# A transformer block's first attention: who inverts the sums of the exponentials

## The chip, the core and the metric

The kernel runs on one core of a Trainium2 chip. A core has five engines with instruction streams of their own: TensorE (PE, matmuls and transposes into PSUM), VectorE (DVE), ScalarE (ACT), GpSimd (POOL) and SyncE (SP, which issues the transfers). They meet only in semaphores: an instruction raises one when it is done, another waits for a value of it. The metric is the time of the whole program on the device in microseconds.

## The reference

Two transformer blocks follow one another on a sequence of 1024 tokens, 1024 wide. Only the attention of the first one bears on the change. It has 8 query heads of 64, and 2 heads of keys and values. Each query block of 128 tokens sees all 1024 keys:

```python
def blocked_gqa(q, k, v):
    q = q * jnp.asarray(1.0 / math.sqrt(HEAD_DIM), q.dtype)
    qb = q.reshape(B, nb, Q_BLOCK, N_KV_HEADS, Q_PER_KV, HEAD_DIM).transpose(1, 0, 2, 3, 4, 5)

    def one_block(qblk):
        s = jnp.einsum('bqkgd,bskd->bkgqs', qblk, k).astype(jnp.float32)
        p = jax.nn.softmax(s, axis=-1).astype(v.dtype)
        return jnp.einsum('bkgqs,bskd->bqkgd', p, v)
...
```

All of it is float32. Before it stand a norm, the input projections and a rotary embedding; behind it the output projection, a gated feed-forward network with a short convolution, and the second block, whose own attention has another shape.

## The kernel before

Almost everything outside the attentions is a large matmul in three products of high and low halves (L746), for which GpSimd splits the weights (L537 to L540).

In the first attention the work is a row of 64 units. A unit is one head of one query block: 128 queries against 1024 keys. Sixteen units (two query blocks) are a pass; three passes run in a hardware loop and the fourth is written out. A unit u goes through these steps:

- TensorE, `scores` (L833): four matmuls of 128x512 into half u%2 of `acc`. They wait until the exponentials of unit u-2 have read that half.
- VectorE, `largest` (L1812): scales the scores in place and finds the bias of the softmax, NBI.
- ScalarE, `exponents` (L1258): the exponentials EX, with their sum in SUM[u%2]. In the trace that is an ACTIVATE and behind it the reading of the accumulator (ACTIVATION_READ_ACCUMULATOR).
- VectorE, `invert_sums` (L1818): RC = 1 / SUM, one element a partition.
- GpSimd, `normalise` (L569, L570): multiplies EX by RC, 16 columns by one form of instruction and 1008 by another.
- TensorE (L863): eight transposes of EX into PSUM, four to a half, in three banks that take turns (`turn`, `bank`). A half needs the bank to be free, that is, the low part PTL of the third half before it.
- ScalarE (L1270) copies a half out rounded, PTH; VectorE (L1842) subtracts to get the low half PTL.
- TensorE, `values` (L848): every second unit sixteen matmuls of PTH and PTL with the values.

Every engine's order is written out by hand, in a loop over u. VectorE at step u: `invert_sums(u+1)`, `largest(u+2)`, at u = 5, 9, 13 the gathering of the output (L1828, L1829), the two halves of PTL of unit u, and at u = 5 and 13 a step of other work (a row of modulations, L1655, here "ADA step"). The fourth gathering stands at the end of the pass. GpSimd at step u: `normalise(u+1)`, then at u = 1 to 3 and 9 to 11 one of three steps in which the queries of the next block are stacked (`stack_queries`: QL at L552, two halves of QST at L560), and at u = 12 and at the end of the pass the low part ML of the output (L587), which waits for the gathered output and ScalarE's rounded copy of it. TensorE takes the units in pairs: for odd u scores(u+2), transposes(u), scores(u+3), transposes(u+1), values(u).

Of the kernel before, what the change touches and what calls it, by code (L numbers as in the profile page):

```python
# [11 lines left out]
ALU = mybir.AluOpType  # L12
# [88 lines left out]
for _name, _w in _VECS:  # L101
    VCOL[_name] = NVEC
    NVEC += _w
_CONSTS = [("ident", 128), ("headmean", 128), ("rot", 128), ("headsel", 2), ("one", 1), ("eps", 1), ("zero", 1), ("edge", 64)]
CCOL, NCONST = {}, 0
for _name, _w in _CONSTS:
    CCOL[_name] = NCONST
# [27 lines left out]
def build(nc, A, out):  # L135
    ctx = ExitStack()
    with ctx:
        BASE = 16512

        def at(name, kb, shape, dt=F32):  # L140
            return nc.alloc_sbuf_tensor_at(name, shape, dt, offset=BASE + int(kb * 1024))

        def sem(name):
            return ctx.enter_context(nc.semaphore(name))
# [16 lines left out]
        EX = [at(f"EX{s}", kb, [P, T]) for s, kb in enumerate((64, 68, 16, 20))]  # L161
# [91 lines left out]
        SUM = at("SUM", small + 1.46875, [P, 8])  # L253
        RC = at("RC", small + 1.5, [P, 8])
# [7 lines left out]
        def con(name, w, j=0):  # L262
            return CON[:, CCOL[name] + j:CCOL[name] + j + w]

        ident, one, eps, zero = con("ident", P), con("one", 1), con("eps", 1), con("zero", 1)
# [33 lines left out]
        scores_done, nb_ready, exp_done, rc_ready, exn_ready = (  # L299
            sem("scores_done"), sem("nb_ready"), sem("exp_done"), sem("rc_ready"), sem("exn_ready"))  # L300
# [27 lines left out]
        def block_of(k):  # L328
            return slice(k, k + 1) if isinstance(k, int) else bass.ds(k, 1)
# [197 lines left out]
        def _(pool):  # L527
# [36 lines left out]

            def normalise(it, u):

                pool.wait_ge(rc_ready, it * 16 + (u + 1))
                x, r = EX[u % 4], RC[:, u % 2:u % 2 + 1]
                pool.tensor_tensor(x[:, 0:FEW], x[:, 0:FEW], r.to_broadcast([P, FEW]), ALU.mult).then_inc(exn_ready, 1)  # L569
                pool.tensor_scalar(x[:, FEW:], x[:, FEW:], r, 1.0, ALU.mult, ALU.mult).then_inc(exn_ready, 1)  # L570

            def attend(it, last):
                for u in range(16):
                    if u < 15 or not last:
                        normalise(it, u + 1)
                    if 1 <= u <= 3:
                        stack_queries(it, 1, u - 1, it * 32 + (2 * u + 4))
                    if 9 <= u <= 11 and not last:
                        stack_queries(it, 2, u - 9, it * 32 + (2 * u + 4))
                    if u == 12:  # L580
                        branch_second(it, 0)
                branch_second(it, 1)
# [8 lines left out]
            for step in range(3):  # L591
                stack_queries(0, 0, step)
            normalise(0, 0)
            with steps.loop(3, 2) as it:
                attend(it, False)
# [987 lines left out]
        def _(dve):  # L1583
# [69 lines left out]
            def modulation(w, cond, out):  # L1653

                ins = dve.scalar_tensor_tensor(out=w, in0=w, scalar=1.0, in1=cond[:, :], op0=ALU.mult, op1=ALU.mult, accum_out=out)  # L1655
                ins.then_inc(ada_used, 1)
# [152 lines left out]
            def largest(it, u):  # L1809
                j = u % 2  # L1810
                dve.wait_ge(scores_done, it * 16 + (u + 1))
                dve.tensor_scalar(acc[:, j, :], acc[:, j, :], column(RSN, it * 16 + u), None, ALU.mult, ALU.min,  # L1812
                                  accum_out=NBI[:, j:j + 1]).then_inc(nb_ready, 1)

            def invert_sums(it, u):
                j = u % 2
                dve.wait_ge(exp_done, it * 16 + (u + 1))
                dve.reciprocal(RC[:, j:j + 1], SUM[:, j:j + 1]).then_inc(rc_ready, 1)  # L1818

            def gather_o(it, b):  # L1820

                dve.wait_ge(otmp_ready, it * 4 + (b + 1))
                g = b % 2
                if g == 0:
                    dve.wait_ge(ml_ready, it * 2 + (b // 2 + 1))
                o = bank6[0:64, :].rearrange("p (i j q) -> p i j q", j=2, q=P)
                m = OTMP[0:64, :].rearrange("p (i j q) -> p i j q", j=2, q=P)
                link(dve.tensor_tensor(OT[0:64, 2 * g:2 * g + 2, :], o[:, :, 0, :], m[:, :, 0, :], ALU.add))  # L1828
                dve.tensor_tensor(OT[64:128, 2 * g:2 * g + 2, :], o[:, :, 1, :], m[:, :, 1, :], ALU.add).then_inc(o_ready, 1)  # L1829

            def attend(it, last):
                for u in range(16):
                    if u < 15 or not last:
                        invert_sums(it, u + 1)
                    if u < 14 or not last:
                        largest(it, u + 2)
                    if u % 4 == 1 and u > 1:
                        gather_o(it, u // 4 - 1)

                    for h in range(2):  # L1840
                        dve.wait_ge(pth_ready, it * 32 + (2 * u + h + 1))
                        dve.tensor_tensor(PTL[:, 4 * h:4 * h + 4, u % 4, :],  # L1842
                                          turns[(2 * u + h) % 3].rearrange("p (k q) -> p k q", q=P),
                                          PTH[:, 4 * h:4 * h + 4, u % 4, :].bitcast(F32), ALU.subtract).then_inc(ptl_ready, 1)
                    if u % 8 == 5:
                        j = u // 8
                        dve.wait_ge(ada3_in[j], it * 16 + 16)
                        modulation(ADA3[j][:, :], C1B, MOD1[:, block_of(it * 2 + (16 + j))])
                gather_o(it, 3)

            dve.wait_ge(cond_ready, 4)
            largest(0, 0)
            largest(0, 1)
            invert_sums(0, 0)
            with steps.loop(3, 4) as it:
                attend(it, False)
            attend(3, True)
            link(dve.tensor_copy(MX[:, 6:7], eps))
            link(dve.tensor_tensor(MOD1[:, 16:24], MOD1[:, 16:24], vec("b_ada", 16, 8), ALU.add))
# [336 lines left out]
def layout(x):  # L2196
# [39 lines left out]
    con = np.zeros((P, NCONST), np.float32)  # L2236
    con[:, CCOL["ident"]:CCOL["ident"] + P] = np.eye(P)
    r = np.arange(P)
    con[:, CCOL["headmean"]:CCOL["headmean"] + P] = (r[:, None] // HD == r[None, :] // HD) / HD
    rot = np.zeros((P, P))  # L2240
# [5 lines left out]
    con[:, CCOL["rot"]:CCOL["rot"] + P] = rot  # L2246
    con[:, CCOL["headsel"]:CCOL["headsel"] + 2] = r[:, None] // HD == np.arange(2)[None, :]
    con[:, CCOL["one"]] = 1.0
    con[:, CCOL["eps"]] = EPS
    for g, w in enumerate(POOL_W):  # L2250
        t = np.r_[0:8, T - 8:T]
# [51 lines left out]
```

## Time and profile before

| | |
|---|---|
| median of 3 runs | 2469.54 us (2466.7 to 2470.85) |
| the profiled execution | 2466.74 us |
| its span | 2465.0 us |
| TensorE busy | 2343.0 us (95%) |
| VectorE busy | 1113.7 us (45%) |
| ScalarE busy | 775.2 us (31%) |
| GpSimd busy | 863.9 us (35%) |
| first attention, from 206 to 418 us: TensorE, VectorE, ScalarE, GpSimd busy | 183.1, 185.8, 163.4, 113.8 us of 212 |

The profile is one execution with the start and length of each instruction. A time in brackets behind an instruction is how long its engine stood idle before it, and what ended that. A row with xN holds several instructions of one form. Busy time of TensorE is that of its matmuls, whose ends are modelled. The span is the time from the first instruction to the last; the execution's own time is a little longer.

### The profile page before, as it was taken

To read this page: it belongs to the slowest core of one execution; us is meant where nothing else is said; L and a number is where in the kernel's file an instruction comes from. 1 tells how busy PE (TensorE), PEld (TensorE's weight loads), DVE (VectorE), ACT (ScalarE), POOL (GpSimd) and SP (SyncE) were. 2 spreads that over 40 slices of the span, in tenths; PEclk is the share of its full clock that TensorE was granted. 3 is DMA by queue.
4 is the path that set the end of the run, shared out by engine and by line. 5 is a ranking of instruction groups with operands and counts; after the bars stand their busy time and mean duration, and the time that the engine had idled before them with its cause. 6 is when DMAs were issued, how large, how long until landed. Compare 5 with 4: busy or idle time off the path is not lost.

```text
span 2465.0 us, 30785 instructions
## 1 busy us (share of the span) xinstructions
PE 2343.0 (95%) x11310; PEld 1924.1 (78%) x11310; DVE 1113.7 (45%) x1381; ACT 775.2 (31%) x1095; POOL 863.9 (35%) x851
## 2 busy tenths in 40 slices
PE   4997888999999999999999999999999999999997
PEld 3776777777888888888778888887778888888886
DVE  7978887479631344124463343352211122222324
ACT  3237776032310222024424454452112111212210
POOL 1445554334433333223223323332223334333331
PEclk9998999999999999999999999999999999999999
DMA  7310001524111111111131111112011111111132
GB/s 305 116 50 28 17 26 49 217 94 179 51 51 43 51 51 43 51 60 49 39 111 61 55 36 54 36 30 91 22 40 44 49 51 52 51 47 41 49 128 77
DMA packets 48318, 166.02 MB, mean 67 GB/s; under 512 B 4480, under 2 KB 6272, under 8 KB 48128
## 3 DMA queue, kind: packets, MB, share of 16 engines
q1 hardware_dynamic: 48256, 165.19, 19.3%
q8 instruction: 39, 0.64, 0.1%
q14 instruction: 23, 0.19, 0.0%
HBM read 156.79 MB, written 8.39 MB: 67 GB/s over the span
## 4 chain that ended last, share of the span: by engine, by line
PE 80%; DVE 9%; issue 4%; ACT 3%; POOL 2%; DMA 1%; SPq 0%; DVEq 0%; ACTq 0%; POOLq 0%
PE acc L746 62%; PE turn L971 6%; PE bank L1035 3%; DVE ADA L1655 1%; DMA WF<-in_w 1%; PE bank L1013 1%; PE acc L959 1%; PE bank L848 1%; DVE HL L1635 1%; DVE acc L1812 1%; PE turn L640 1%; ACT EX L1258 1%; PE acc L724 1%; PE bank L1110 1%; PE bank L1107 1%
## 5 line engine op out<-in xcount | busy, mean ns | idle before, releaser
L746 PE MATMUL acc<-HH,WH 128*128 128x512 f32 x1600 | 497.4, 392 | 7.3 <-POOL WL L540 6.3
L746 PE MATMUL acc<-HL,WH 128*128 128x512 f32 x1600 | 493.9, 390 | 0.0
L746 PE MATMUL acc<-HH,WL 128*128 128x512 f32 x1600 | 493.8, 390 | 0.0
L537 POOL TENSOR_TENSOR WH<-WF,CON 128x16 fp32r<-128x16 f32 x186 | 52.7, 284 | 1206.1 <-PE acc L746 1024.5
L540 POOL TENSOR_TENSOR WL<-WF,WH 128x1024 fp32r<-128x1024 f32 (+2 forms) x186 | 439.5, 2363 | 15.5
L746 PEld LDWEIGHTS acc<-HH,WH 128*128 128x128 f32 x1600 | 300.5, 188 | 74.0 <-issue 6.9
L746 PEld LDWEIGHTS acc<-HL,WH 128*128 128x128 f32 x1600 | 301.3, 188 | 62.8
L746 PEld LDWEIGHTS acc<-HH,WL 128*128 128x128 f32 x1600 | 301.1, 188 | 62.8
L538 POOL TENSOR_SCALAR WH<-WF 128x1008 fp32r<-128x1008 f32 (+2 forms) x186 | 195.4, 1050 | 0.0
L1942 DVE SCALAR_TENSOR_TENSOR CV<-EV,VEC,CV 128x1023 f32<-128x1023 f32 x44 | 99.1, 2253 | 203.9 <-ACT CV L1334 203.1
L1870 DVE SCALAR_TENSOR_TENSOR XT<-acc,MOD,XT 128x1024 f32 (+1 forms) x34 | 43.6, 1284 | 233.1 <-PE acc L746 233.1
L1332 ACT ACTIVATE EV<-acc 128x1024 f32<-128x1024 f32 x44 | 45.2, 1027 | 282.6 <-PE acc L746 276.7
L2127 DVE TENSOR_TENSOR CV<-EV,EV 128x1024 f32<-128x1024 f32 x16 | 33.5, 2096 | 185.5 <-ACT EV L1559 185.5
L746 PE MATMUL acc<-GH,WH 128*128 128x512 f32 x340 | 106.0, 393 | 4.3 <-DVE GL L1958 3.7
L746 PE MATMUL acc<-GL,WH 128*128 128x512 f32 x340 | 105.2, 391 | 0.0
L746 PE MATMUL acc<-GH,WL 128*128 128x512 f32 x340 | 105.2, 390 | 0.0
L2015 DVE TENSOR_TENSOR acc<-acc,BIAS 128x384 f32<-128x384 f32 x64 | 36.1, 564 | 143.0 <-PE acc L962 142.8
L611 POOL TENSOR_TENSOR EX<-EX,RC 128x16 f32<-128x16 f32 x64 | 13.9, 217 | 231.7 <-DVE RC L2021 231.6
L1035 PE MATMUL bank<-PT,VTOK 128*64 128x128 f32 x640 | 84.6, 280 | 0.4 <-DVE CBF L2031 0.4
L1812 DVE TENSOR_SCALAR_CACHE_REDUCE acc<-acc,RSN 128x1024 f32<-128x1024 f32 x64 | 82.3, 1287 | 3.0 <-PE acc L833 0.5
L1258 ACT ACTIVATE EX<-acc,NBI 128x1024 f32<-128x1024 f32 x64 | 71.5, 1117 | 30.6 <-DVE acc L1812 30.0
L746 PEld LDWEIGHTS acc<-GH,WH 128*128 128x128 f32 x340 | 63.9, 189 | 19.0 <-DVE GL L1958 4.9
(373 smaller groups left out, 4100.2 us busy)
## 6 DMA issues: line engine op xcount, KB each, us to landing
WF<-in_w SPq DMA_DIRECT2D x150, 512.0 KB, 3.4
ADA<-in_ada SPq DMA_DIRECT2D x15, 1024.0 KB, 13.1
BIAS<-in_bias SPq DMA_DIRECT2D x16, 576.0 KB, 3.8
XT<-in_xT SPq DMA_DIRECT2D x16, 512.0 KB, 10.2
ADA<-in_ada SPq DMA_DIRECT2D x4, 2048.0 KB, 11.6
ADA<-in_ada SPq DMA_DIRECT2D x3, 2560.0 KB, 9.3
WF<-in_w SPq DMA_DIRECT2D x24, 256.0 KB, 2.6
ADA<-in_ada SPq DMA_DIRECT2D x8, 512.0 KB, 3.4
```

Source lines behind the costliest of these rows:

```text
L537: pool.tensor_tensor(h[:, 0:FEW], f[:, 0:FEW], zero.to_broadcast([P, FEW]), ALU.add).then_inc(w_hi, 1)
L538: pool.tensor_scalar(h[:, FEW:k * P], f[:, FEW:k * P], 1.0, 1.0, ALU.mult, ALU.mult).then_inc(w_hi, 1)
L540: pool.tensor_tensor(WL[slot][:, 0:k, :], WF[slot][:, 0:k, :], WH[slot][:, 0:k, :].bitcast(F32), ALU.subtract).then_inc(w_split, 1)
L746: last = pe.matmul(acc[:, slot, HALF * c:HALF * c + HALF], w[slot][:, k, :], x[:, k, HALF * c:HALF * c + HALF], start=(k == 0 and w is WH ...
L971: mm = pe.matmul(turn[:, HALF * c:HALF * c + HALF], w[slot][:, k, :], x[:, k, HALF * c:HALF * c + HALF], start=(k == 0 and w is WH and x i ...
L1035: mm = pe.matmul(bank7[0:HD, P:2 * P], VTOK2[:, j, kc, :], PT2[u % 2][:, P * k:P * k + P], start=(k == 0), stop=(k == NKEY // P - 1))
L1258: act.activation(EX[u % 4][:, :], acc[:, u % 2, :], ACT.Exp, bias=NBI[:, u % 2:u % 2 + 1], scale=-1.0, accum_out=SUM[:, u % 2:u % 2 + 1]). ...
L1332: act.activation(EV[s][:, :], acc[:, s, :], ACT.Copy).then_inc(act_step, 1)
L1812: dve.tensor_scalar(acc[:, j, :], acc[:, j, :], column(RSN, it * 16 + u), None, ALU.mult, ALU.min, accum_out=NBI[:, j:j + 1]).then_inc(nb_ ...
L1870: dve.scalar_tensor_tensor(out=x, in0=acc[:, s, :], scalar=gate(it * 2 + s), in1=x, op0=ALU.mult, op1=ALU.add).then_inc(acc_read, 1)
L1942: link(dve.scalar_tensor_tensor(out=CV[s][:, 1:T], in0=EV[s][:, 0:T - 1], scalar=vec("conv_w", f), in1=CV[s][:, 1:T], op0=ALU.mult, op1=AL ...
L2015: link(dve.tensor_tensor(a[:, P:P + NLOC], a[:, P:P + NLOC], BIAS[g % 2][:, KIND[c], :], ALU.subtract))
```

## The change

GpSimd computes the inverse itself: `normalise` now waits for the exponentials (`exp_done`), raises SUM to the power of -1 (a new constant, one column `minus` of the table of constants), waits for its own result through the same semaphore `rc_ready`, and multiplies as before. `invert_sums` and its calls are gone from VectorE's stream. The second attention keeps its reciprocals on VectorE.

```diff
-_CONSTS = [("ident", 128), ("headmean", 128), ("rot", 128), ("headsel", 2), ("one", 1), ("eps", 1), ("zero", 1), ("edge", 64)]
+_CONSTS = [("ident", 128), ("headmean", 128), ("rot", 128), ("headsel", 2), ("one", 1), ("eps", 1), ("zero", 1), ("edge", 64), ("minus", 1)]
...
             def normalise(it, u):
 
+                x, r = EX[u % 4], RC[:, u % 2:u % 2 + 1]
+                pool.wait_ge(exp_done, it * 16 + (u + 1))
+                pool.tensor_tensor(r, SUM[:, u % 2:u % 2 + 1], con("minus", 1), ALU.pow).then_inc(rc_ready, 1)
                 pool.wait_ge(rc_ready, it * 16 + (u + 1))
-                x, r = EX[u % 4], RC[:, u % 2:u % 2 + 1]
...
-            def invert_sums(it, u):
-                j = u % 2
-                dve.wait_ge(exp_done, it * 16 + (u + 1))
-                dve.reciprocal(RC[:, j:j + 1], SUM[:, j:j + 1]).then_inc(rc_ready, 1)
-
...
                 for u in range(16):
-                    if u < 15 or not last:
-                        invert_sums(it, u + 1)
                     if u < 14 or not last:
                         largest(it, u + 2)
...
             largest(0, 1)
-            invert_sums(0, 0)
```

GpSimd's stream in a pass, from the normalising of unit 2 to that of unit 4, with the stacking between (EX_63 to EX_66 are the four tiles of exponentials, QST_56 the stacked queries). Before:

```order
L569 TENSOR_TENSOR EX_65<-EX_65,RC 128x16 [waits rc_ready]
L570 TENSOR_SCALAR EX_65<-EX_65,RC 128x1008
L551 ISA
L552 ISA [waits qh_ready]
L552 TENSOR_TENSOR QL<-QN,QH 128x512
L567 REGISTER_ALU
L569 TENSOR_TENSOR EX_66<-EX_66,RC 128x16 [waits rc_ready]
L570 TENSOR_SCALAR EX_66<-EX_66,RC 128x1008
L558 ISA [waits pool_step]
L560 TENSOR_TENSOR QST_56<-QL,CON 64x4x128 [waits exn_ready]
```

And changed:

```order
L571 TENSOR_TENSOR EX_65<-EX_65,RC 128x16 [waits rc_ready]
L572 TENSOR_SCALAR EX_65<-EX_65,RC 128x1008
L551 ISA
L552 ISA [waits qh_ready]
L552 TENSOR_TENSOR QL<-QN,QH 128x512
L568 REGISTER_ALU
L569 TENSOR_TENSOR RC<-SUM,CON 128x1 [waits exp_done]
L571 TENSOR_TENSOR EX_66<-EX_66,RC 128x16 [waits rc_ready]
L572 TENSOR_SCALAR EX_66<-EX_66,RC 128x1008
L558 ISA [waits pool_step]
L560 TENSOR_TENSOR QST_56<-QL,CON 64x4x128 [waits exn_ready]
```

The power (L569) stands between QL and the multiplication, and the wait for the exponentials is now GpSimd's; what follows is as it was.

VectorE's stream in the same pass, one step of a unit. Before:

```order
L1818 RECIPROCAL RC<-SUM 128x1 [waits exp_done]
L1811 REGISTER_ALU
L1812 ISA [waits scores_done]
L1812 TENSOR_SCALAR acc,NBI<-acc,RSN 128x1024
L1841 REGISTER_ALU
L1842 TENSOR_TENSOR PTL<-bank,PTH 128x4x128 [waits pth_ready]
```

And changed:

```order
L1813 REGISTER_ALU
L1814 ISA [waits scores_done]
L1814 TENSOR_SCALAR acc,NBI<-acc,RSN 128x1024
L1836 REGISTER_ALU
L1837 TENSOR_TENSOR PTL<-bank,PTH 128x4x128 [waits pth_ready]
```

The reciprocal and its wait are gone; the minimum waits for the scores alone.

## Rows read from the trace of the kernel before

**Rows 1.** The page: a line of part 1, one of part 5.
```profile
PE 2343.0 (95%) x11310; PEld 1924.1 (78%) x11310; DVE 1113.7 (45%) x1381; ACT 775.2 (31%) x1095; POOL 863.9 (35%) x851
...
L540 POOL TENSOR_TENSOR WL<-WF,WH 128x1024 fp32r<-128x1024 f32 (+2 forms) x186 | 439.5, 2363 | 15.5
```

**Rows 2.** Windows: stretch, length, busy PE, PEld, DVE, ACT, POOL, clock, DMA.
```profile
206.00:418.00 212.00, 183.09 (x1245) 157.81 (x1243) 185.81 (x358) 163.44 (x293) 113.77 (x153) 0.99 0.05 15
```

**Rows 3.** What TensorE waited for, 206 to 418: total us, times, longest.
```profile
PE bank L863 <- POOL EX L570: 11.4, 6, 3.3
PE turn L863 <- POOL EX L570: 6.1, 14, 0.6
PE turn L863 <- DVE PTL L1842: 6.0, 8, 0.8
PE bank L863 <- DVE PTL L1842: 3.1, 4, 0.8
PE bank L848 <- DVE PTL L1842: 2.9, 3, 1.0
```

**Rows 4.** By time, an even stretch: start, length, engine, line.
```profile
286.99 0.19 ACT L1258 ACTIVATION_READ_ACCUMULATOR EX<-acc,NBI 128x1 f32 x1
...
287.22 0.16 DVE L1818 RECIPROCAL RC<-SUM 128x1 f32<-128x1 f32 x1
287.44 1.29 DVE L1812 TENSOR_SCALAR_CACHE_REDUCE acc<-acc,RSN 128x1024 f32<-128x1024 f32 x1
287.46 0.22 POOL L569 TENSOR_TENSOR EX<-EX,RC 128x16 f32<-128x16 f32 x1 [1.53 <-DVE RC L1818]
...
290.06 0.16 DVE L1818 RECIPROCAL RC<-SUM 128x1 f32<-128x1 f32 x1
```

**Rows 5.** By time, GpSimd and TensorE where a pass begins and behind the stackings.
```profile
263.01 0.22 POOL L569 TENSOR_TENSOR EX<-EX,RC 128x16 f32<-128x16 f32 x1
...
264.37 0.66 PE L863 MATMUL bank<-CON,EX 128*128 128x128 f32 x4 [3.25 <-POOL EX L570]
...
267.97 1.30 POOL L552 TENSOR_TENSOR QL<-QN,QH 128x512 f32<-128x512 f32 x1 [2.39 <-ACT QH L1250]
...
270.58 1.09 PE L863 MATMUL turn<-CON,EX 128*128 128x128 f32 x8 [0.48 <-POOL EX L570]
...
271.80 0.22 POOL L569 TENSOR_TENSOR EX<-EX,RC 128x16 f32<-128x16 f32 x1 [0.16 <-POOL QST L560]
...
273.16 0.66 PE L863 MATMUL bank<-CON,EX 128*128 128x128 f32 x4 [0.56 <-POOL EX L570]
...
298.78 1.09 PE L863 MATMUL turn<-CON,EX 128*128 128x128 f32 x8 [0.35 <-POOL EX L570]
...
319.37 0.66 PE L863 MATMUL bank<-CON,EX 128*128 128x128 f32 x4 [3.23 <-POOL EX L570]
```

**Rows 6.** By time, units 7 and 8 of the same pass.
```profile
276.47 0.62 PE L833 MATMUL acc<-KSL,QST 128*128 128x512 f32 x2
...
277.25 1.29 DVE L1812 TENSOR_SCALAR_CACHE_REDUCE acc<-acc,RSN 128x1024 f32<-128x1024 f32 x1
...
285.99 0.66 PE L863 MATMUL turn<-CON,EX 128*128 128x128 f32 x4 [0.38 <-POOL EX L570]
```

**Rows 7.** By time, VectorE at the end of the pass.
```profile
309.19 0.68 DVE L1842 TENSOR_TENSOR PTL<-bank,PTH 128x512 fp32r<-128x512 f32 x1
...
310.22 1.29 DVE L1812 TENSOR_SCALAR_CACHE_REDUCE acc<-acc,RSN 128x1024 f32<-128x1024 f32 x1
```

**Rows 8.** By time, ScalarE at the start of the first pass.
```profile
198.25 1.28 ACT L1258 ACT_TABLE_LOAD   x1
...
210.99 1.11 ACT L1258 ACTIVATE EX<-acc,NBI 128x1024 f32<-128x1024 f32 x1 [0.48 <-DVE acc L1812]
```

**Rows 9.** By time, the end of the last pass.
```profile
416.35 0.16 DVE L1818 RECIPROCAL RC<-SUM 128x1 f32<-128x1 f32 x1
...
417.95 1.09 PE L863 MATMUL turn<-CON,EX 128*128 128x128 f32 x8 [0.64 <-POOL EX L570]
```

More of the change, by code:

```diff
@@ L2248, in layout @@
     con[:, CCOL["one"]] = 1.0
+    con[:, CCOL["minus"]] = -1.0
     con[:, CCOL["eps"]] = EPS
```

## The prediction, made before the changed kernel ran

> **What bounds the kernel now.** I read the page first for the whole, then the stretch of the first attention (206 to 418 us) by windows, by what TensorE waited for, and by time. TensorE is busy 95% of the whole span [rows 1], but in the first attention it is busy 183.1 us of 212 [rows 2]: 29 us of gaps. The list of waits says what ended them: 17.5 us for a normalised tile of exponentials from GpSimd (11.4 + 6.1, 20 times) and 12.0 us for the low halves PTL from VectorE (6.0 + 3.1 + 2.9, 15 times) [rows 3]. Nowhere else does the change touch anything, so no more than these 29.5 us can be had, and what they grow by is the loss.
>
> A pass of sixteen units takes 55.0 us (the gaps at 264.37 and 319.37) [rows 5], and its gaps are few and fixed in place: one of 3.25 us where a pass begins, two of 0.48 and 0.56 us behind the stacking of queries in units 1 to 3, one of 0.35 behind the second stacking [rows 5], one of 0.38 in unit 8 [rows 6], and, between them, waits for PTL of 0.8 to 0.95 us [rows 3]. In the even stretches between, one unit follows another on VectorE after 2.84 us (reciprocals at 287.22 and 290.06) [rows 4]. There the profile shows a ring: the sums are read out at 286.99, the reciprocal starts at 287.22, the next minimum (L1812) at 287.44, and only from that minimum can the next exponentials come [rows 4]. So the 0.16 us of the reciprocal occupy 0.22 us of VectorE's queue, and, more than that, they hold the next minimum until the exponentials before it are done. But TensorE itself is busy 183.1 / 64 = 2.86 us a unit [rows 2], so the ring of 2.84 alone costs next to nothing. Only the gaps count.
>
> **The change part by part.** *Taken from VectorE*: 64 reciprocals of 0.16 us, and the wait for the exponentials. *Added to GpSimd*: 64 powers on 128x1, and a wait for its own semaphore before each normalisation. The constants grow by one column of 128 values, which come in the same transfer at the start: nothing.
>
> Call c what a unit pays on GpSimd: the power p and the own wait w. The trace has no power. Below, p is bounded by the reciprocal, 0.16 us [rows 4]; nearest is GpSimd's own small operation, the 128x16 multiplication: 0.22 us [rows 4]; above, by GpSimd's largest operation in this stretch, 1.30 us for 128x512 (QL), since a power is many steps but on one element per partition [rows 5]. I take p = 0.30: the small operation, and half as much again for steps that a multiplication doesn't have. Twice that or more is well possible. For w there are two rows: the 0.16 us between a stacked query and the multiplication behind its wait [rows 5], and the 15.5 us over 186 splits, 0.08 each, before L540, which waits for L538 in the same manner [rows 1]. I take 0.16, since the rows of this stretch show it. c = 0.46, with 0.24 to 1.45 as ends.
>
> The Trainium skill (GPSIMD Engine Reference, § 4.1 Engine selection) says to give elementwise work to VectorE, GpSimd being some two times slower; on one element no row here can show that. By its factor on the reciprocal p would be 0.33, and the total below would be 0.7 us more.
>
> Now one pass, gap by gap, as the shift of TensorE against before. "Queued" means that GpSimd already has work in a row and the sums have long been there: the whole c is added. "Waiting" means that GpSimd is idle and follows the exponentials: there c takes the place of the 0.24 us from the start of the reciprocal (287.22) to that of the multiplication (287.46) [rows 4].
>
> - *Start of a pass.* Unit 1 is normalised only behind the subtraction ML (L587), which waits for the last values of the pass before; its multiplication stands at 263.01, right at that subtraction's end, and TensorE stands idle until 264.37 for it [rows 5]. The power is queued between: + c.
> - *Units 3 and 4.* GpSimd does QL, normalises 3, stacks, normalises 4, stacks, without a break and both transposes wait for it (270.58 and 273.16) [rows 5]: + 2c. Unit 2 has 0.6 us to spare (its transposes come 0.6 behind GpSimd) and unit 5 over 1, so they add nothing while c stays under 0.6. So far + 3c.
> - *Unit 7 to 8.* The scores of unit 7 end at 276.47 + 0.47 = 276.94, its minimum starts at 277.25, because of the reciprocal in front [rows 6]. That 0.3 goes. Behind it hang the gathering of O, PTL of unit 5 (the wait of 0.78), the ADA step and the minimum of unit 8, before which a further 0.08 of a reciprocal goes: - 0.38. Then unit 8 is normalised, waiting: + c - 0.24. Its transposes at 285.99 follow GpSimd [rows 6]. Together c - 0.62.
> - *Units 11 and 12.* The second stacking, again queued; unit 12's transposes at 298.78 waited for it [rows 5]: + 2c.
> - *End of a pass.* VectorE's second half of PTL ends at 309.19 + 0.68 = 309.87; the next minimum starts at 310.22, behind exponentials and reciprocal [rows 7], and PTL of unit 15 and the values wait on it. It now starts 0.35 earlier, and the 0.3 of the minimum of unit 15, before the gathering, is gone as for unit 7: - 0.67.
>
> A middle pass: 3c + (c - 0.62) + 2c - 0.67 = 6c - 1.29, and there are two. The first pass has no subtraction ahead of it; unit 0 is waiting (c - 0.24), and the exponentials of unit 3, which stood 0.48 us for the minimum [rows 8], need not: 3c - 0.72 in place of 3c, in all 6c - 2.01. The last pass has no second stacking; in it the transposes of unit 15 wait 0.64 for GpSimd, because the reciprocal stood at 416.35 behind an ADA step long after its exponentials [rows 9]: that gap goes, and the 0.3 of a minimum before it: 3c + c - 0.62 - 0.3 - 0.64 = 4c - 1.56.
>
> The sum: 22c - 6.15. With c = 0.46: 10.1 - 6.15 = + 4.0 us. Even at c = 0.28; + 0.2% (4.9 us) at c = 0.50. The price is paid six times a middle pass, because GpSimd, idle for 98 of the 212 us [rows 2], is busy in just the places where TensorE waits for it.
>
> The profiled execution took 2466.74 us (span 2465.0), the median of three runs is 2469.54; the difference of 4 us belongs to either: 2470.7 for the one, 2473.5 for the other. I forecast the median.
>
> **The rivals.**
>
> *Case 1, as summed, p up to 0.34.* c = 0.24 to 0.50: - 0.9 to + 4.9 us, 2468.7 to 2474.4. For it: GpSimd's small operations all take about 0.2 us.
>
> *Case 2, slower: the power is dear.* If p is 0.34 to 0.8, c is 0.5 to 0.96: + 4.9 to + 15.7 by the formula (over 0.62 unit 2 adds c - 0.62 per pass: 1.2 us more). At p = 1.29 or so, c = 1.45: + 25.8, and some 3 for unit 2: 2498. One mechanism, at one place: GpSimd's row from QL to the second stacked half, twice a pass. It decides from c = 0.50. For it: a power in floating point is a long run of steps, and nothing in the trace says that these are few. Against the far end: only one element per partition.
>
> *Case 3, faster: VectorE's freedom is worth more than I count.* Each wait of TensorE for PTL (12.0 us) [rows 3] hangs on VectorE, which is busy 186 of the 212 us [rows 2]. The sum lets a third of them go. If all 12.0 went, with the 0.64 of unit 15, the 0.48 of the start and 0.24 at each of the five waiting places, against 22c: 10.1 - 12.0 - 0.64 - 0.48 - 1.2 = - 4.2 us at my c, - 7.7 at c = 0.30: 2462 to 2465.5. Against it: most of these waits come from the gathering of O and from the scores of that unit, which come from TensorE, not from the reciprocal.
>
> *Case 4, a price paid once.* The first power stands directly before the first transposes of the attention. If its code had to be fetched first, the first pass would be later by that, once. The nearest row is ScalarE's table load ahead of the first exponentials, 1.28 us [rows 8]: + 1.3 on the sum, 2474.8. The Trainium skill (GPSIMD Engine Reference, § 2.1 Instruction dispatch) gives about 6 us for the first call of a newly loaded kernel on GpSimd; by that it would be + 10. No row shows such a load on GpSimd, and a tensor_tensor with another operation need not be one.
>
> **How the numbers follow.** About 0.2% or 4.9 us is what a measurement of this kernel can tell from no change. Case 1 0.46 (within), case 2 0.43 (slower; of it 0.10 over + 16 us), case 3 0.06 (faster), case 4 0.05 (0.03 within, 0.02 slower). Faster 0.06, same 0.49, slower 0.45. Likeliest: 2473.5. Case 1's own range is 2467.5 to 2475. The range that holds 8 in 10 leaves out case 3 and the far part of case 2: 2467.5 to 2489.
>
> **What would show it.** The power's row and the distance from it to the multiplication give c directly; 22c - 6.15 is the sum. Right: the transposes at a pass's start wait 3.2 + c, those behind the stackings 0.5 + c, no minimum stands behind exponentials in the even stretches, and GpSimd's busy time rises by 64p. VectorE's minima should follow the end of PTL or of the scores. Wrong: if the waits for PTL all but vanish (case 3), if TensorE waits for GpSimd in even stretches too (c over 1.2), or if a single long gap stands at the first power (case 4).

## The result, and the profile after

The changed kernel takes 2479.94 us (median of 5, 2477.02 to 2483.82), the kernel before 2469.09 us in the same comparison (2466.6 to 2470.85). The ratio is 1.0048, with a 95% interval of 1.0033 to 1.0062: slower by 10.9 us. The point forecast was 2473.5; the result is case 2 (the power is dear), not the case that I called likeliest.

The power is 0.55 us long, as the instructions that write or read RC show (shortest/median/longest in ns, first and last start):

```profile
L569 POOL TENSOR_TENSOR RC<-SUM,CON x64: 548/550/561, 204.0 to 427.0; 128x1 f32<-128x1 f32 x64
L571 POOL TENSOR_TENSOR EX<-EX,RC x64: 217/217/1300, 204.7 to 427.7; 128x16 f32<-128x16 f32 x64
```

What TensorE waited for in the attention (206 to 428 us here) stands against [rows 3]; GpSimd is the releaser for 27.3 us in place of 17.5, VectorE for 7.5 in place of 12.0:

```profile
PE bank L865 <- POOL EX L572: 15.1, 7, 3.9
PE turn L865 <- POOL EX L572: 12.2, 17, 1.4
PE turn L865 <- DVE PTL L1837: 6.0, 8, 0.8
PE bank L850 <- DVE PTL L1837: 1.5, 3, 0.5
```

By time, the begin of the second pass and its first stacking (start, length), against [rows 5]:

```profile
265.35 0.55 POOL L569 TENSOR_TENSOR RC<-SUM,CON 128x1 f32<-128x1 f32 x1
...
265.98 0.22 POOL L571 TENSOR_TENSOR EX<-EX,RC 128x16 f32<-128x16 f32 x1
...
267.34 1.11 PE L865 MATMUL bank<-CON,EX 128*128 128x128 f32 x4 [3.87 <-POOL EX L572]
...
278.21 0.66 PE L865 MATMUL bank<-CON,EX 128*128 128x128 f32 x4 [1.19 <-POOL EX L572]
```

From the power's start to the multiplication's it is 0.63 us: that is the c of the prediction, p = 0.55 and w = 0.08. The gap at the begin of the pass grew from 3.25 to 3.87 us, by just this, and the one behind the stacking, before unit 4, from 0.56 to 1.19. One thing stands there that I had not forecast: the four transposes behind the gap take 1.11 us, where they took 0.66. The window of the changed kernel that begins 0.34 us ahead of these transposes (length; busy PE, PEld, DVE, ACT, POOL; clock):

```profile
267.00:270.00 3.00, 2.66 (x11) 2.47 (x12) 1.04 (x4) 1.26 (x3) 2.10 (x4) 0.54 0.00 0
```

and of the kernel before, 0.37 us ahead of its transposes of unit 1:

```profile
264.00:267.00 3.00, 2.63 (x20) 2.41 (x21) 2.64 (x5) 1.94 (x3) 1.58 (x3) 1.00 0.00 0
```

TensorE came out of the gap at half its clock (1.2 of 2.4 GHz; a window that holds both levels shows a mean, as the 0.54). In the changed kernel's profile this happens behind all three gaps between passes, in that of the kernel before behind one.

For the rest I compare a middle pass, from the first value matmul of unit 15 to the next such. I divide it into five parts by the starts of the transposes T of the units 1, 4, 8 and 12 and of the values V of unit 15; us:

| | V to T(1) | to T(4) | to T(8) | to T(12) | to V | pass |
|---|---|---|---|---|---|---|
| before | 7.23 | 8.79 | 12.83 | 12.79 | 13.39 | 55.03 |
| changed | 7.86 | 10.87 | 13.19 | 13.85 | 12.89 | 58.66 |
| difference | +0.63 | +2.08 | +0.36 | +1.06 | -0.50 | +3.63 |
| the sum's term at c = 0.63 | +0.63 | +1.26 | +0.01 | +1.26 | -0.67 | +2.49 |

The four passes, the first counted from the first exponentials; us:

| | first | second | third | last |
|---|---|---|---|---|
| before | 54.48 | 55.03 | 55.01 | 52.84 |
| changed | 56.79 | 58.66 | 58.67 | 55.33 |
| difference | +2.31 | +3.63 | +3.66 | +2.49 |
| the sum's term at c = 0.63 | +1.77 | +2.49 | +2.49 | +0.96 |

The stage, from the first exponentials to the first matmul of the output projection, is 223.2 us before (202.66 to 425.83) and 235.3 after (202.69 to 437.96). The profiled executions themselves differ by 14.2 us, since the rest of the program, which is the same, took 2 us more in this one; the medians differ by 10.9. Below, "stage" is always this stretch of a kernel's profiled execution. The rest of the program takes 2240.1 to 2247.6 us in the profiled executions of all kernels here, so for a difference of a few us the stage tells more than the time of one execution.

### The profile page after: what moved, and what is told of

The parts are those of the page before. It is cut to its first block, busy times and chain, and to the rows that moved or that the text cites. A ratio compares the mean times of both kernels' runs of the same rounds, so it can differ in the third digit from the quotient of the medians.

```text
span 2479.2 us, 30782 instructions
## 1 busy us (share of the span) xinstructions
PE 2349.1 (95%) x11310; PEld 1930.0 (78%) x11310; DVE 1106.3 (45%) x1317; ACT 776.1 (31%) x1095; POOL 909.1 (37%) x915
## 4 chain that ended last, share of the span: by engine, by line
PE 81%; DVE 8%; POOL 3%; ACT 3%; issue 3%; DMA 1%; SPq 0%; DVEq 0%; ACTq 0%; POOLq 0%
PE acc L748 61%; PE turn L973 6%; PE bank L1037 3%; PE bank L850 1%; DVE ADA L1657 1%; DMA WF<-in_w 1%; PE bank L1015 1%; POOL EX L572 1%; PE acc L961 1%; PE turn L642 1%; PE acc L835 1%; PE turn L865 1%; PE acc L726 1%; PE acc L684 1%; DVE HL L1637 1%
## 5 line engine op out<-in xcount | busy, mean ns | idle before, releaser
L537 POOL TENSOR_TENSOR WH<-WF,CON 128x16 fp32r<-128x16 f32 x186 | 54.5, 293 | 1208.3 <-PE acc L748 1027.4
L1334 ACT ACTIVATE EV<-acc 128x1024 f32<-128x1024 f32 x44 | 45.2, 1027 | 285.7 <-PE acc L748 279.9
L1156 ACT ACTIVATE SQ<-XT 128x1024 f32 (+1 forms) x21 | 22.3, 1062 | 179.5 <-DVE XT L1864 153.6
```

What stands on the lines that cost most here:

```text
L537: pool.tensor_tensor(h[:, 0:FEW], f[:, 0:FEW], zero.to_broadcast([P, FEW]), ALU.add).then_inc(w_hi, 1)
L1334: act.activation(EV[s][:, :], acc[:, s, :], ACT.Copy).then_inc(act_step, 1)
```

## The experiments

Each ran together with the kernel before on one chip; for the first four that kernel's median was 2470.17 us. My theory was the sum's: GpSimd's queue, six times a pass. The rivals: VectorE's freedom has an effect of its own (for better or worse), and TensorE's clock. A third stood in my expectations: the meeting of GpSimd's multiplication with the ADA step.

### A product in place of the power

```diff
-                pool.tensor_tensor(r, SUM[:, u % 2:u % 2 + 1], con("minus", 1), ALU.pow).then_inc(rc_ready, 1)
+                pool.tensor_tensor(r, SUM[:, u % 2:u % 2 + 1], con("minus", 1), ALU.mult).then_inc(rc_ready, 1)
```

> The changed kernel with a product in place of the power (the result is left wrong: minus the sum stands where its inverse should): same queue, same waits, another operation on the same 128x1. If the loss comes from what a unit pays on GpSimd (c, from the start of the power to that of the multiplication, is 0.63 us in the changed kernel), c falls to about 0.27 (0.19 + 0.08), and the sum 22c - 6.15 gives -0.2 us: 2469 in place of 2479.9. If it comes from the order (VectorE no longer paces, GpSimd's small multiplication now falls together with VectorE's ADA step and takes 1.3 us there), the time stays within 2 us of the changed kernel, 2478 to 2480.

Measured: 2475.12 us (2469.17 to 2481.7), ratio 1.0022 (1.0011 to 1.0033), stage 231.0. The product takes 0.19 us and c is 0.27, as expected. That is about half of the loss, but neither theory had this number: a pass is still 57.4 us. The VectorE rows by time show what goes with it:

```profile
283.51 2.02 DVE L1657 SCALAR_TENSOR_TENSOR ADA<-ADA,C1B 128x1024 f32<-128x1024 f32 x1
...
285.46 1.28 DVE L1814 TENSOR_SCALAR_CACHE_REDUCE acc<-acc,RSN 128x1024 f32<-128x1024 f32 x1
```

The ADA step, 1.22 us in the kernel before, takes 2.02, and the minimum of unit 8 waits behind it. The third and the fifth part of the pass, where the ADA steps are, are 13.64 and 13.68 us long, 0.81 and 0.29 more than before. GpSimd's long multiplication had begun 0.17 us earlier and ended at 284.46; the step ends 1.07 us after that, so nearly all of its 1.22 us came behind it:

```profile
283.34 1.12 POOL L572 TENSOR_SCALAR EX<-EX,RC 128x1008 f32<-128x1008 f32 x1
```

### No inversion at all

```diff
-                x, r = EX[u % 4], RC[:, u % 2:u % 2 + 1]
+                x, r = EX[u % 4], SUM[:, u % 2:u % 2 + 1]
                 pool.wait_ge(exp_done, it * 16 + (u + 1))
-                pool.tensor_tensor(r, SUM[:, u % 2:u % 2 + 1], con("minus", 1), ALU.pow).then_inc(rc_ready, 1)
-                pool.wait_ge(rc_ready, it * 16 + (u + 1))
...
-                pool.wait_ge(rc_ready, u0 + (64 + u + 1))
+                pool.wait_ge(rc_ready, u0 + (u + 1))
```

The last two lines are the second attention's, whose count of reciprocals now begins at 0.

> The changed kernel without any inversion: GpSimd waits for the exponentials and multiplies by the sums themselves (the division of the softmax is left out). This is c = 0 and shows what VectorE's relief is worth at most. The sum says -6 us against the kernel before (2463). If VectorE's relief is worth more than I count (all waits for PTL gone), -10 or more, under 2459.5. If the collision of the small multiplication with the ADA step costs on the path, no more than -3.

Measured: 2473.25 us (2464.76 to 2475.51), ratio 1.0010 (1.0001 to 1.0019); stage 222.3, a middle pass 55.08. The third expectation has the number right (no more than -3): without any inversion on either engine the kernel isn't faster. Whether for its reason, the meeting, is taken up below. Most of the - 6 of my sum was not there to be had in this order. The parts of the pass: 7.21, 8.78, 13.10, 12.58, 13.41. The third and the fifth, where I had put the gains, are those with the ADA step, which here took 1.75 us (the step in full, and the long multiplication beside it):

```profile
278.46 1.12 POOL L570 TENSOR_SCALAR EX<-EX,SUM 128x1008 f32<-128x1008 f32 x1
278.90 1.75 DVE L1655 SCALAR_TENSOR_TENSOR ADA<-ADA,C1B 128x1024 f32<-128x1024 f32 x1
```

The median of this kernel lies above that of its profiled run by 8.5 us; the profile shows no more than the stage of one of the quickest runs, and why the others are longer it can't tell.

### Two powers

```diff
+                pool.tensor_tensor(RC[:, 4:5], SUM[:, u % 2:u % 2 + 1], con("minus", 1), ALU.pow)
                 pool.tensor_tensor(r, SUM[:, u % 2:u % 2 + 1], con("minus", 1), ALU.pow).then_inc(rc_ready, 1)
```

> The changed kernel with each power computed twice, the first into an unused column: c rises by 0.52 to 0.55 us. By the slope of the sum, 22 us for each us of c, +12 us, and 2 more for unit 2, whose slack of 0.6 is used up: 2492 to 2494. If GpSimd's queue binds only at the begin of a pass and the rest of the loss is TensorE's clock, which fell to 0.50 for 3 to 6 us behind the 3.87 us gap, then only +2 to +4: 2482 to 2484.

Measured: 2494.28 us (2493.92 to 2496.99), ratio 1.0100 (1.0085 to 1.0116); stage 249.9, 14.6 more than the changed kernel for 0.55 us more of c. The queue theory holds here: 14.6 us stand against the 12 of the slope and 2 for unit 2. The two middle passes are 62.2 and 61.4 us long, each with a gap of 4.38 us at its begin and a fall of the clock behind it, a shorter one in the second of them.

### The changed kernel, ML later

GpSimd normalises unit 1 of the next pass ahead of the subtraction ML:

```diff
                 for u in range(16):
-                    if u < 15 or not last:
+                    if 0 < u < 15 or (u == 15 and not last):
                         normalise(it, u + 1)
...
+                if not last:
+                    normalise(it, 17)
                 branch_second(it, 1)
...
             normalise(0, 0)
+            normalise(0, 1)
```

> The changed kernel with one step moved: the normalising of a pass's second unit stands before the subtraction ML of the pass before, where GpSimd stood idle 4.4 us. The 3.87 us gap before the transposes of unit 1 goes, and the fall of the clock behind it. But unit 2's exponentials set unit 2's transposes, so a part comes back: I expect 2.7 us a pass, -8 us in all, 2472, and a clock near 1.0 all through. If the clock has no part in it and unit 2 takes the gap over whole, -1 us a pass, 2477.

Measured: 2473.41 us (2470.02 to 2481.16), ratio 1.0015 (1.0005 to 1.0024); stage 228.5, a pass 56.2 in place of 58.7. That is - 2.5 us for each pass but the first, close to the 2.7 expected (second 56.18, third 56.15, last 52.72); the first, which has no ML ahead of it, is 0.9 longer (57.65). So the stage gains 6.8 us. TensorE's clock doesn't fall at any of the three places. At 6 us into the pass TensorE now waits for PTL, and from the transposes of unit 4 on nothing is different (13.20, 13.85 and 12.89 us to units 8, 12 and the values):

```profile
266.56 0.66 PE L868 MATMUL turn<-CON,EX 128*128 128x128 f32 x4 [1.62 <-DVE PTL L1840]
```

### The kernel before, ML later

The same edit without the change.

> The kernel before, reciprocals on VectorE, with the same one step moved as in the run before: GpSimd normalises a pass's second unit ahead of the subtraction ML of the pass before. The reciprocal of that unit stands behind the gathering of O on VectorE (260.99 in the trace of before), so the multiplication can begin at 261.2 in place of 263.0. I expect the 3.25 us gap to shrink by 1.8, half of it to come back in unit 2, and -1 us a pass, -3 in all: 2466 to 2467. If the gap is set by the gathering alone, nothing.

Measured: 2466.14 us (2462.78 to 2471.21) against 2469.41, ratio 0.9991 (0.9982 to 1.0000); stage 220.9, a pass 54.4 (- 0.6). The gap of 3.25 us shrank by 1.8, and two thirds of it came back, a little more than I had thought: 1.46 remain in front of unit 1, and unit 2 now waits 0.38.

### No inversion, ADA step later

On top of the kernel without inversion, the ADA step goes from behind PTL of unit 5 (and 13) to behind the minimum of unit 8 (and 16):

```diff
                     if u < 14 or not last:
                         largest(it, u + 2)
+                    if u % 8 == 6:
+                        j = u // 8
+                        dve.wait_ge(ada3_in[j], it * 16 + 16)
+                        modulation(ADA3[j][:, :], C1B, MOD1[:, block_of(it * 2 + (16 + j))])
...
-                    if u % 8 == 5:
-                        j = u // 8
-                        dve.wait_ge(ada3_in[j], it * 16 + 16)
-                        modulation(ADA3[j][:, :], C1B, MOD1[:, block_of(it * 2 + (16 + j))])
```

> The kernel without any inversion, with VectorE's ADA step (two operands in SBUF) moved from before the minimum of units 8 and 16 to behind it, where GpSimd has finished its long multiplication. Without the move the ADA step took 1.75 us in place of 1.22 wherever it met that multiplication, and a pass lasted 55.1 us, no less than before. If that meeting ate what VectorE's relief is worth, the ADA step is back at 1.22 and a pass falls to 54 or less, the stage from 222.3 to 218. If the relief is worth nothing because TensorE's scores come late anyway, a pass gains only what the earlier minimum of unit 8 gives, under 0.5 us.

Measured: 2465.02 us (2462.11 to 2466.82) against 2469.41, ratio 0.9981 (0.9972 to 0.9990); stage 219.2, a pass 54.5. The ADA step is back at 1.22 us in seven of its eight places; in the eighth it still meets the multiplication and takes 1.76.

The stage is 3.1 us shorter than with the step in its old place, a pass 0.56. That alone doesn't show what the meeting cost. The same move in a kernel whose reciprocals are on VectorE, where the two had never met, takes 0.45 us from a pass (54.40 to 53.95) and 1.8 from the stage, as the runs with ML later and with both moves show. So, as far as the two kernels compare, about 0.1 us a pass is left for the meeting. For the same reason the 0.51 us between this pass and that of the kernel before can come from the place of the ADA step, and not from VectorE's relief. The number of the first expectation, 54 us or less and a stage of 218, was not reached.

### The changed kernel, ADA step later

> The changed kernel with the ADA step moved in the same manner. In the changed kernel the small multiplication began in the same instant as the ADA step and took 1.3 us in place of 0.22 in all eight places. Moved, it should be 0.22 everywhere, unit 8 should not be waited for (0.82 us), and unit 8's and 16's minima come 1.2 us earlier: -1 to -1.5 us a pass, -5 in all, 2474 to 2476. If the collision is off the path, within 1 us of the changed kernel.

The same edit of the ADA step, on the changed kernel. Measured: 2480.56 us (2478.0 to 2481.48), ratio 1.0043 (1.0029 to 1.0056): no different from the changed kernel. The stage is 2.1 us shorter (233.2), the wait of 0.82 us before unit 8 became 0.17, and the multiplication takes 0.22 us at seven of the eight places. But the medians don't show it (in the profiled execution the rest of the program took 1.7 us more than in the changed kernel's). The time I expected, 2474 to 2476, is a miss.

### The kernel before, both moves

> The kernel before with both moves. If the two add up, -3 from the first and -2 to -4 from the ADA step: 2463 to 2465, faster than both kernels. If the ADA step only moves the wait from one unit to the next, no different from the first move alone.

Measured: 2465.09 us (2462.41 to 2468.74) against 2469.41, ratio 0.9985 (0.9976 to 0.9994). Stage 219.1, a pass 53.9. The two moves add in the stage (- 2.3 and - 1.8); the time is at the upper end of what was expected, 1 us less than with the first move alone (2466.14).

### The power only where nobody waits for GpSimd

The change undone for the units 1, 3, 4, 8, 11 and 12 of each pass, with a semaphore of its own for the powers:

```diff
...
+ON_POOL = [0, 2, 5, 6, 7, 9, 10, 13, 14, 15]
+ON_DVE = [1, 3, 4, 8, 11, 12]
...
-                pool.wait_ge(rc_ready, it * 16 + (u + 1))
                 x, r = EX[u % 4], RC[:, u % 2:u % 2 + 1]
+                if u % 16 in ON_POOL:
+                    pool.wait_ge(exp_done, it * 16 + (u + 1))
+                    pool.tensor_tensor(r, SUM[:, u % 2:u % 2 + 1], con("minus", 1), ALU.pow).then_inc(pw_ready, 1)
+                    pool.wait_ge(pw_ready, turn_of(it, u, ON_POOL))
+                else:
+                    pool.wait_ge(rc_ready, turn_of(it, u, ON_DVE))
...
             def invert_sums(it, u):
+                if u % 16 in ON_POOL:
+                    return
```

> The change undone in part: in each pass the units 1, 3, 4, 8, 11 and 12, whose transposes TensorE waits for, get their inverse from VectorE as before; the other ten keep the power on GpSimd. If the loss is c times the places where GpSimd's row is waited for, all of it goes: a pass of 54.9 to 55.3 us in place of 58.7, the stage 222 to 224 in place of 235, 2469 to 2470. If it is a matter of GpSimd's total work or of the meeting with the ADA step (units 7 and 15, still there), ten sixteenths of the loss stay, 2475 or more.

Measured: 2470.62 us (2462.88 to 2472.36) against 2470.31, ratio 0.9999 (0.9990 to 1.0008); stage 223.1. The whole loss is gone, with forty of the sixty-four powers still on GpSimd. A pass is 54.38 us: 7.22, 8.78, 12.76, 12.73, 12.89, that is before's in the first four parts and the changed kernel's in the last. The gain that I had put at the end of a pass is real. The run also answers for the meeting: GpSimd's small multiplication begins together with the ADA step and takes 1.27 to 1.30 us at all eight places, as in the changed kernel, and yet nothing is lost. So this meeting has no visible part in the 10.9 us.

This kernel also gives the clock's price by itself, since its second and third pass are the same work. Behind the gap of the second (windows as above) the clock held, behind that of the third it did not:

```profile
263.00:269.00 6.00, 5.12 (x38) 4.69 (x39) 4.29 (x8) 4.70 (x11) 4.17 (x7) 1.00 0.00 0
```

```profile
318.00:324.00 6.00, 5.75 (x24) 5.26 (x25) 3.73 (x7) 4.29 (x8) 3.35 (x6) 0.51 0.00 0
```

By time, the transposes of unit 1 and GpSimd's QL behind them, in both passes:

```profile
263.88 0.66 PE L877 MATMUL bank<-CON,EX 128*128 128x128 f32 x4 [3.24 <-POOL EX L584]
...
267.47 1.29 POOL L561 TENSOR_TENSOR QL<-QN,QH 128x512 f32<-128x512 f32 x1 [1.75 <-ACT QH L1264]
...
318.25 1.12 PE L877 MATMUL bank<-CON,EX 128*128 128x128 f32 x4 [3.23 <-POOL EX L584]
...
322.67 1.28 POOL L561 TENSOR_TENSOR QL<-QN,QH 128x512 f32<-128x512 f32 x1 [2.58 <-ACT QH L1264]
```

The pass with the full clock is 54.38 us long (256.66 to 311.04), the other 55.61 (311.04 to 366.65). The first 0.83 us of these 1.23 are there when QL starts: 4.42 us behind the transposes in place of 3.59. GpSimd can't start QL before ScalarE's QH, and in ScalarE's order QH stands behind the copies PTH of these transposes, and the second copy came 2.00 us behind them in place of 1.18. So a slow TensorE delays the very row that it then waits for. Not every fall costs as much: with no inversion the second pass had none and the third had one that began over 1 us behind the transposes, and they are 55.08 and 55.30 us long; with both moves they are 53.95 and 53.93. The gap in front was the same here, 3.24 and 3.23 us, so its length alone doesn't decide.

### Both moves, and the power for unit 1 alone

> The kernel before with both moves, and the power on GpSimd for unit 1 of each pass alone, where GpSimd stands idle for the rounded output: its price is hidden there, and unit 1 no longer waits for the reciprocal behind the gathering (a wait of 1.45 us). I expect 0.4 us a pass over the two moves alone, the stage 218 in place of 219.1, 2464. If TensorE then waits for PTL instead, as it did for 1.6 us with the power everywhere, no gain.

The kernel before with both moves (ML and the ADA step later), and on top of them the power for unit 1 of each pass, ON_POOL = [1]. Measured: 2465.09 us (2462.15 to 2467.34) against 2470.31, ratio 0.9978 (0.9969 to 0.9987). Stage 219.0, a pass 53.9: nothing over the two moves alone (219.1). The wait of 1.46 us for GpSimd became one of 1.6 for PTL, as the second expectation had it.

With the two moves alone the interval is nearly the same (0.9976 to 0.9994); both intervals lie below 1, and the power has no part in it that can be seen.

## Why the prediction was right, and where not

**The mechanism was right.** The time lies in the range, in case 2 and not at the likeliest value. The price is paid in GpSimd's row at the six places that were named: with the power left out of these six the loss is 0 (0.9999), with the power doubled it is more than double (1.0100). The begin of a pass took + 0.63 for c = 0.63, and the run with the six units undone has the first two parts of a pass as before, to 0.01 us. It undid all six at once, so what each is worth by itself is not shown; the waits before units 1 and 4 grew by c each.

**The price of the power was mis-sized.** I took p = 0.30 from the small multiplication (0.22) and half as much again; it is 0.55, two and a half times the multiplication. My reason (a power is many steps, but on one element) gave no number, and no run shows what steps it takes, and I still put the likeliest case on the cheap side. The wait w is 0.08, the row of the weight splitting, not the 0.16 behind a stacked query. c is 0.63 in place of 0.46. By the sum that makes + 7.7 us in place of + 4.0. Measured are + 10.9, which leaves 3.2 us; in the profiled executions, whose stages differ by 12.1, it leaves 4.4, and the next points are read from these. So with the right c the sum would have given about seven tenths of the loss. That the time fell into the range is owed to the width that I gave to the power's price, which had to hold these 3.2 us as well. A slip in case 2: the formula gives + 15.0 at c = 0.96, and 16.2 with unit 2, not 15.7.

**The gain at unit 7 was not there.** I took 0.3 us from the distance between the end of the scores and the minimum [rows 6], because of the reciprocal in front. In the changed kernel no reciprocal is in front, and the minimum still starts 0.3 us after TensorE goes on to the next transposes (281.98, and 276.92 before):

```profile
281.52 0.62 PE L835 MATMUL acc<-KSL,QST 128*128 128x512 f32 x2
281.98 0.60 PE L865 MATMUL turn<-CON,EX 128*128 128x128 f32 x4
...
282.30 1.29 DVE L1814 TENSOR_SCALAR_CACHE_REDUCE acc<-acc,RSN 128x1024 f32<-128x1024 f32 x1 [1.47 <-PE acc L835]
```

That is the way from a matmul to whoever waits for it. I had read an end as a start of somebody's wait by adding the spacing of matmuls, and called the rest a gain. This goes with the 0.35 between + 0.01 and + 0.36 in the third part, which is there in all four passes (0.36, 0.35, 0.36, 0.42), 1.5 us together. What I had put at the end of a pass came: - 0.50 for - 0.67, and - 0.50 again with the six units undone.

**The last pass.** Here the sum had + 0.96 and the trace has + 2.49. At its end I had let 0.94 us go, and 0.28 went. The wait before unit 15 fell from 0.64 to 0.33, but the one before unit 14 grew from 0.59 to 1.45. Unit 14 is normalised behind the subtraction ML of step 12, in every pass, so its power is queued too: a seventh place that I had not named. In the middle passes TensorE waits 0.62 us there, and nothing is lost by it: the run with the six units undone has the same wait, and the last part of its pass is as short as the changed kernel's. In the last pass it costs.

**The clock was missing.** Of the + 2.08 in the second part, 1.26 is 2c. The other 0.82 is the delay of QL: in the changed kernel QL starts 4.42 us behind the transposes of unit 1 in both middle passes, in the kernel before 3.60 (264.37 and 267.97 [rows 5]).

```profile
271.76 1.29 POOL L552 TENSOR_TENSOR QL<-QN,QH 128x512 f32<-128x512 f32 x1 [2.58 <-ACT QH L1252]
```

These are the two figures of the run with the six units undone, 4.42 with the fall and 3.59 without. So the clock took 1.6 us in the two middle passes. With the 1.5 of unit 7 and the 0.7 at the end of the last pass that is 3.8 of the 4.4 us; the last pass also has 0.45 too much up to unit 4, with a fall of the clock in both kernels, which I didn't follow further.

The clock fell behind three gaps in place of one. That a longer gap makes the fall likelier is supported by a count over all profiles, three gaps between passes in each: behind gaps of 1.4 to 1.6 us it fell at 3 of 12 (the changed kernel, ML later, 0; the kernel before, ML later, 1; both moves 1; the same with the power for unit 1, 1), behind gaps of 3.23 to 3.25 us at 8 of 12 (the kernel before 1, without inversion 2, the same with the ADA step later 3, with the six units undone 2), and behind gaps of 3.5 to 4.4 us at 12 of 12 (the product, the changed kernel, the same with the ADA step later, two powers). What decides between two gaps of the same length is open, and the share of the clock in the median of the runs can't be read from one profile of each.

**The rivals.** Case 3, VectorE's freedom worth 12 us, is refuted: with no inversion anywhere and the ADA step out of the way the stage falls by 4.0 us (223.2 to 219.2), and moving the ADA step gave 1.8 of such a fall with the reciprocals in place. Case 4, a price paid once, did not show: the first power, at 204.0, is among the 64 of 548 to 561 ns. The Trainium skill's factor of two for GpSimd (GPSIMD Engine Reference, § 4.1 Engine selection) gives p an estimate of 0.33 from the reciprocal; the trace has 0.55, so the direction agrees, and the factor against the reciprocal's 0.16 is 3.4. GpSimd's busy time rose by 45.2 us (863.9 to 909.1), more than 64p = 35.2: the small multiplications that met the ADA step, eight of up to 1.30 us in place of 0.22, are some 8.5 of the rest. The waits behind the stackings became 0.5 + c only before units 4 and 12 (1.19 us); before units 3 and 11 they are 0.37 and 0.20. Of the signs of being wrong, a wait for GpSimd in an even stretch below c = 1.2, none came: the 0.62 us stand at unit 14, behind ML.

## What to carry to other kernels

An instruction moved to an idle engine costs at the places where somebody already waits for that engine, so count these places first and price the instruction second; here, with six units in sixteen relieved of it, the whole loss was gone. A price that no row shows deserves the middle of its range, not the row nearest to its cheap end. Ask also what a longer wait does to the waiting engine: here its clock fell, and it came back late to the row it waits for. And the distance between a producer's modelled end and its consumer's start is no slack until a run shows it to be.

## What the runs showed of the hardware

**VectorE and GpSimd held each other up** in this kernel where VectorE read two operands from SBUF, so they do not meet only in semaphores. In the changed kernel the small multiplication and the ADA step begin in the same instant, and it is GpSimd that stands: 1.30 us in place of 0.22, with VectorE's 1.22 untouched.

```profile
285.60 1.30 POOL L571 TENSOR_TENSOR EX<-EX,RC 128x16 f32<-128x16 f32 x1
285.60 1.22 DVE L1657 SCALAR_TENSOR_TENSOR ADA<-ADA,C1B 128x1024 f32<-128x1024 f32 x1
```

With the product and without inversion GpSimd's long multiplication came first, by 0.17 and 0.44 us, and VectorE stood: 2.02 and 1.75 us, in both cases to 1.07 us behind the multiplication's end. With both moves the multiplication was 0.83 us ahead, and the step took 1.35 us. VectorE's minimum, which reads `acc` in PSUM, stands beside a small multiplication in the kernel before, and both keep their length, 1.29 and 0.22 us [rows 4]. In the kernel before, the ADA step and GpSimd's multiplications never met, since the reciprocal that released GpSimd stood behind the ADA step. The Trainium skill has this (GPSIMD Engine Reference, § 8 Key points: contention with VectorE instructions "with two SBUF inputs"; SBUF — State Buffer, section SBUF: two separate sides, calls it an exclusive lock for whoever starts first), and the traces agree: 2.02, 1.75 and 1.30 us where each alone takes 1.22, 1.22 and 0.22. I had read it and not asked which instruction would come to lie beside which once the reciprocal no longer kept them apart.

**A power on GpSimd**, 128x1 float32, takes 0.55 us, a product in its place 0.19, VectorE's reciprocal 0.16.

**TensorE's clock** fell to half (1.2 of 2.4 GHz) behind 3 of 12 gaps of 1.4 to 1.6 us, 8 of 12 of 3.2 us and 12 of 12 of 3.5 us and more. A fall cost from nothing to 1.2 us of a pass.
